# A 31-tap depthwise convolution on one engine in place of two

## The reference, cut to what matters

```python
def conformer_conv_mixer(h_conv, dw_w, dw_b, ln_g, ln_b):
    a, g = jnp.split(h_conv, 2, axis=-1)          # 256 channels each
    u = a * jax.nn.sigmoid(g)
    u = depthwise_conv(u, dw_w, dw_b)             # 31 taps per channel
    return jax.nn.silu(layernorm(u, ln_g, ln_b))
```

## Time and profile before

| | |
|---|---|
| median of 3 runs | 3576.89 us (3570.51 to 3579.43) |
| profiled execution | 3579.76 us, span of its trace 3577.9 us |
| TensorE matmul busy | 3313.3 us, 93% |
| VectorE busy | 1830.2 us, 51% |
| GpSimd busy | 1969.5 us, 55% |
| ScalarE busy | 758.2 us, 21% |
| mean granted TensorE clock | 0.965 of full |

### The profile page before, as it was taken

One profiled execution on the slowest core, in us unless ns is written; L12 is line 12 of the kernel. 1 busy time (PEld: TensorE's weight loads), 2 busy tenths in 40 slices (PEclk: granted clock), 3 DMA queues, 4 the chain that ended last, 5 costly groups with the idle time before them and its releaser, 6 DMA issues.

```text
span 3577.9 us, 44532 instructions
## 1 busy us (share of the span) xinstructions
PE 3313.3 (93%) x14288; PEld 2588.7 (72%) x14288; DVE 1830.2 (51%) x2038; ACT 758.2 (21%) x1269; POOL 1969.5 (55%) x1148
## 2 busy tenths in 40 slices
PE   7999997799999999996889999888898899999997
PEld 5888773378887788874457888667776777778886
DVE  6641367653313743157654331765668766853313
ACT  2110124422201111013432210211123222222201
POOL 4556654356666546665426666533344445666664
PEclk9999998899999999998899999989999999999998
DMA  4223320023333223330013332312122122233332
GB/s 138 77 83 94 112 71 12 7 72 98 96 98 112 89 71 95 94 106 30 12 36 94 94 99 94 103 53 64 59 68 65 59 71 71 86 92 100 94 95 76
DMA packets 77136, 280.89 MB, mean 79 GB/s; under 512 B 9350, under 2 KB 9734, under 8 KB 76360
## 3 DMA queue, kind: packets, MB, share of 16 engines
q1 hardware_dynamic: 74016, 268.84, 24.6%
q10 hardware_dynamic: 2984, 10.27, 0.9%
HBM read 276.97 MB, written 2.10 MB: 78 GB/s over the span
## 4 chain that ended last, share of the span: by engine, by line
PE 78%; DVE 15%; issue 4%; ACT 2%; DVEq 0%; ACTq 0%; POOL 0%; DMA 0%; SPq 0%; POOLq 0%
PE bank L547 23%; PE bank L552 23%; PE bank L551 23%; DVE y L1872 1%; DVE xbc L2164 1%; PE bank L811 1%; PE bank L672 1%; DVE x_lo L1630 1%; PE bank L829 1%; PE bank L754 1%; DVE ssm_lo L1784 1%; DVE square_sum L1640 1%; DVE scaled L1994 1%; PE bank L742 1%; PE bank L1027 1%
## 5 line engine op out<-in xcount | busy, mean ns | idle before, releaser
L447 POOL TENSOR_SCALAR w_hi<-raw 128x1024 fp32r<-128x1024 f32 x504 | 554.6, 1100 | 1523.2 <-PE bank L547 1514.4
L450 POOL TENSOR_TENSOR w_lo<-raw,w_hi 128x1024 fp32r<-128x1024 f32 x504 | 1266.1, 2512 | 42.0
L547 PE MATMUL bank<-x_hi,w_hi 128*128 128x512 f32 x2896 | 1159.7, 400 | 86.7 <-DVE x_lo L1630 30.0
L551 PE MATMUL bank<-x_lo,w_hi 128*128 128x512 f32 x2896 | 1141.8, 394 | 0.0
L552 PE MATMUL bank<-x_hi,w_lo 128*128 128x512 f32 x2896 | 1141.5, 394 | 0.0
L547 PEld LDWEIGHTS bank<-x_hi,w_hi 128*128 128x128 f32 x2896 | 553.0, 191 | 228.7 <-issue 99.9
L551 PEld LDWEIGHTS bank<-x_lo,w_hi 128*128 128x128 f32 x2896 | 553.5, 191 | 119.3 <-issue 5.1
L552 PEld LDWEIGHTS bank<-x_hi,w_lo 128*128 128x128 f32 x2896 | 552.2, 191 | 118.1
L552 PE MATMUL bank<-hidden_hi,w_lo 128*128 (+1 forms) x880 | 347.6, 395 | 0.0
L547 PE MATMUL bank<-hidden_hi,w_hi 128*128 (+1 forms) x880 | 347.6, 395 | 0.0
L551 PE MATMUL bank<-hidden_lo,w_hi 128*128 (+1 forms) x880 | 347.6, 395 | 0.0
(11 more groups left out here) (373 smaller groups left out, 3407.0 us busy)
## 6 DMA issues: line engine op xcount, KB each, us to landing
raw<-in_w SPq DMA_DIRECT2D x504, 512.0 KB, 3.6
dft<-in_dft ACTq DMA_DIRECT2D x2, 1536.0 KB, 6.9
x<-in_x SPq DMA_DIRECT2D x2, 1024.0 KB, 6.6
out<-x SPq DMA_DIRECT2D x4, 512.0 KB, 2.6
mask<-in_mask ACTq DMA_DIRECT2D x1, 1536.0 KB, 8.2
filt_cos<-in_dft_filter ACTq DMA_DIRECT2D x2, 512.0 KB, 6.1
filt_sin<-in_dft_filter ACTq DMA_DIRECT2D x2, 512.0 KB, 7.2
sel<-in_sel ACTq DMA_DIRECT2D x1, 768.0 KB, 4.4
```

Source lines behind the costliest of these rows:

```text
L447: nc.gpsimd.tensor_scalar(w_hi[:, s % 2, :], raw[:, s, :], 1.0, 0.0, ALU.mult, ALU.add).then_inc(w_rounded, 1)
L450: nc.gpsimd.tensor_tensor(w_lo[:, s % 2, :], raw[:, s, :], w_hi[:, s % 2, :].bitcast(F32), ALU.subtract).then_inc(w_split, 1)
L547: first = nc.tensor.matmul(out, hi_w, hi, start=start, stop=False)
L551: nc.tensor.matmul(out, hi_w, lo, start=False, stop=False)
```

## The change

GpSimd no longer computes any tap: `long_conv`, its two semaphores and the scratch tiles go, and GpSimd's list for the whole program up to the second block is weight splits alone. VectorE computes all 62 taps of a layer, alternating between the two tiles: tap number n belongs to tile n % 2, and waits for the previous tap of its own tile, for which `tap_at` now has two entries. `maximum` issues two taps behind each row maximum while there are any, and its scaling waits for the maximum alone and no longer for a tap. `fold` and `spectrum_sums` still issue one. `branches_done` no longer waits for GpSimd. The loop over the layers counts 180 steps of `dve_step` in place of 149.

```diff
-    "dve": {"pair_free": 44, "tile_free": 14, "dve_step": 149, "x_rounded": 24, "x_split": 24, "x_squared":
+    "dve": {"pair_free": 44, "tile_free": 14, "dve_step": 180, "x_rounded": 24, "x_split": 24, "x_squared":
...
-        tap_products = (rstd[:], latent[:, 2, :])
...
-            def long_conv(l, first, end):
...
-                def tap(j):
-                    return issue(nc.gpsimd.tensor_scalar(tap_products[j % 2], long_pad[:, 0, j:j + T],
-                                                         layer_cols[:, CONV_W + j:CONV_W + j + 1], 0.0,
-                                                         ALU.mult, ALU.add))
...
-                for j in range(first, end):
-
-                    pool.wait_ge(long_tap, added)
-                    this = product
-                    if j + 1 < end:
-                        product = tap(j + 1)
-                    pool.wait_ge(long_tap, max(this, added))
-                    added = issue(nc.gpsimd.tensor_tensor(acc, acc, tap_products[j % 2], ALU.add))
...
-            for l in range(LAYERS):
-
-                end = l * LAYER_BLOCKS + FFN_BLOCKS + IN_BLOCKS + 2
-                split_blocks(at, end)
-                long_conv(l, 0, TAPS // 2)
-                split_blocks(end, end + 2)
-                long_conv(l, TAPS // 2, TAPS)
-                at = end + 2
-
...
-                taken, tap_at = [0], [None]
+                taken, tap_at = [0], [None, None]

                 def long_tap():

-                    j = taken[0]
+                    i, j = taken[0] % 2, taken[0] // 2
                     taken[0] += 1
                     if j:
-                        dve.wait_ge(dve_step, tap_at[0])
-                    acc, w, src = conv_acc[:, 1, :], col(CONV_W + TAPS + j), long_pad[:, 1, j:j + T]
+                        dve.wait_ge(dve_step, tap_at[i])
+                    acc, w, src = conv_acc[:, i, :], col(CONV_W + i * TAPS + j), long_pad[:, i, j:j + T]
                     if j == 0:
-                        ins = nc.vector.tensor_scalar(acc, src, w, col(CONV_B + 1), ALU.mult, ALU.add)
+                        ins = nc.vector.tensor_scalar(acc, src, w, col(CONV_B + i), ALU.mult, ALU.add)
                     else:
                         ins = nc.vector.scalar_tensor_tensor(acc, src, w, acc, ALU.mult, ALU.add)
                     ins.then_inc(dve_step, c.add(dve_step))
-                    tap_at[0] = c.at(dve_step)
+                    tap_at[i] = c.at(dve_step)

                 def tap():
-                    if taken[0] < TAPS:
+                    if taken[0] < 2 * TAPS:
                         long_tap()
...
-                def maximum(h, t, tap=True):
+                def maximum(h, t):
                     dve.wait_ge(scores_ready, c.next(scores_ready))
                     nc.vector.reduce_max(row_shift[:, t:t + 1], bank[SCORE_BANKS[(4 * h + t) % 3]][:], AX_X
                                          ).then_inc(dve_step, c.add(dve_step))
-                    if tap and taken[0] < TAPS:
-                        long_tap()
-                    dve.wait_ge(dve_step, c.at(dve_step))
+                    reduced = c.at(dve_step)
+                    tap()
+                    tap()
+                    dve.wait_ge(dve_step, reduced)
                     nc.vector.tensor_scalar(row_shift[:, t:t + 1], row_shift[:, t:t + 1],
                                             -QK ** -0.5, None, ALU.mult).then_inc(row_ready, c.add(row_ready))
...
-                while taken[0] < TAPS:
+                while taken[0] < 2 * TAPS:
                     long_tap()
-                dve.wait_ge(dve_step, tap_at[0])
+                dve.wait_ge(dve_step, tap_at[1])

                 def branches_done():
                     y_update(1, 0)
-                    dve.wait_ge(long_done, c.next(long_done))
                     dve.sem_inc(ln_in, 1)
```

More of the change, by code:

```diff
@@ L110 @@
            "q_ready": 8, "q_roped": 8, "scores_ready": 32, "row_ready": 40, "probs_ready": 32,
-           "mixed_ready": 8, "mixed_copied": 8, "long_done": 1, "spec_free": 4, "filt_loaded": 48,
-           "odd_copied": 8, "spec_taken": 4, "k_copied": 4},
+           "mixed_ready": 8, "mixed_copied": 8, "spec_free": 4, "filt_loaded": 48, "odd_copied": 8,
+           "spec_taken": 4, "k_copied": 4},
 }
@@ L389, in build @@
         gate_in, gate_out = sem("gate_in"), sem("gate_out")
-        long_tap, long_done = sem("long_tap"), sem("long_done")
         norm_in, norm_squared, norm_summed, norm_sum, norm_rms, norm_scaled, norm_rounded, norm_split = (
@@ L461, in split_blocks @@
                     split_block(n, n // RAW, n % RAW, True)
-            def long_conv(l, first, end):
[L465 to L472, removed]
-                def tap(j):
-                    return issue(nc.gpsimd.tensor_scalar(tap_products[j % 2], long_pad[:, 0, j:j + T],
-                                                         layer_cols[:, CONV_W + j:CONV_W + j + 1], 0.0,
-                                                         ALU.mult, ALU.add))
[L479 to L487, removed]
-                for j in range(first, end):
-                    pool.wait_ge(long_tap, added)
-                    this = product
-                    if j + 1 < end:
-                        product = tap(j + 1)
-                    pool.wait_ge(long_tap, max(this, added))
-                    added = issue(nc.gpsimd.tensor_tensor(acc, acc, tap_products[j % 2], ALU.add))
-                pool.wait_ge(long_tap, added)
-                if end == TAPS:
-                    pool.sem_inc(long_done, 1)
             for n in range(RAW):
```

## The result

| | before | after |
|---|---|---|
| median | 3578.16 us (3570.51 to 3582.34, 4 runs) | 3557.06 us (3553.68 to 3561.33, 4 runs) |
| profiled execution | 3579.76 us, span 3577.9 | 3557.09 us, span 3555.3 |
| ratio, 95% interval | | 0.9948 (0.9934 to 0.9962) |

By the medians that is 21.1 us or 0.6% less, by the ratio 18.6 us or 0.5%. Two repetitions beside the experiments gave 14.4 us less (ratio 0.9957, 0.9941 to 0.9973) and 17.2 us less (0.9953, 0.9941 to 0.9966). One of the six executions of the second repetition took 11595 us; the ratio leaves it out, and without it that median is 3559.20 and not 3559.34. The forecast was 14.2 us less, 3563 us, in a range of 3554 to 3571.

The account below looks back on a forecast made before the run. TensorE was busy 93% of the span, but GpSimd's work stretched VectorE's instructions in the attention heads; steps sum to -8.8 us per layer, +1.7 for a slow clock spell, -14.2 for both layers: 3563 us, range 3554 to 3571.

Parts of the forecast that it names:

- rival D: Stretched VectorE instructions are not GpSimd's doing: 12.3 us lost per layer, 3601.5 us; chance 0.05.
- Step (1): Query rotations, two rounds: eight sums fall from 0.93 to 0.69 us each, 1.9 us saved per layer.
- Step (2): Maxima of score head 0: 9.50 us becomes 8.34, 1.2 us saved per layer.
- Steps (3) and (7): head(0) and head(4): first reduce to last scaling falls from 18.76 and 20.66 to 14.07 us, saving 4.7 and 6.6.
- Step (4): head(1): three second taps ahead of the spectrum TensorE waits for, 1.3 us lost per layer.
- Step (5): head(2): four second taps, each ahead of a `y_update` or the exponentials, 1.7 us lost per layer.
- Step (6): head(3): TensorE's transform and ScalarE's copy set its end and the maxima have slack; no change beyond the rotations.
- Step (8): head(5), which had no taps: slower first pitch and later scalings of the second and third maxima, 2.6 us lost.
- C: Each second tap costs the full 0.90 us, as if waited for: +3.5 us per layer, 3584 us; chance 0.06.
- E: VectorE isn't the whole path in head(0) and head(4), half their saving goes: 3574 us; chance 0.07.
- A: TensorE's clock holds in head(5), or slow spells elsewhere vanish: 3559 us, or 3556 with one fewer per layer; chance 0.17.
- B: More slow TensorE clock spells, as waits in head(2) grow: one more per layer 3566 us, two 3569.5; chance 0.17.

Follow-up runs that it names:

- without taps on GpSimd: Kernel before with one of GpSimd's 31 tile-0 taps kept and 30 left out of the computation, VectorE's taps and waits as before: 3539.96 us, ratio 0.9901.
- the busy GpSimd beside the changed kernel: Changed kernel with GpSimd's 61 instructions per layer put back on scratch tiles, result unused: 3609.13 us, ratio to before 1.0098.
- the kernel with 62 taps in waits: Changed kernel with its 62 taps laid elsewhere, many where VectorE waits, up to six together, some ahead of query rotations: 3531.87 us, ratio to before 0.9885.

## Why the prediction was right

The sum was right within the scatter (-14.2 against -14.4, -17.2 and -21.1 us) and so was the mechanism: silence on GpSimd shortens VectorE's instructions, the second taps give part of it back. That the sum came so close is partly luck, because both of these terms were too large. Below, the sizes of the steps, for one layer. Lengths of heads are from first maximum to first maximum in the first layer, of before, then of the three profiles of the changed kernel.

- **The silence.** Forecast by rival D's arithmetic: 19.4 us, of them 0.95 in the first round of rotations, which lies ahead of the stretch. Measured without taps on GpSimd: 16.8 by half the whole time, and 14.6 and 14.0 in the two stretches, for 18.4. The parts at head(0) and head(4) were right in the first layer (6.4 and 8.3 forecast, 6.4 and 8.1 measured); score head 0 gave 1.9 and not 2.8, because its fourth maximum then waits 1.08 us for TensorE, and head(3) and head(5) lost 2.6 together. In the second layer head(4) gave only 6.2, head(1) lost 1.2, and head(3) and head(5) lost nothing: before the change, head(3) and head(4) share their 41 us differently in the two layers (14.59 + 26.44 and 16.15 + 24.67).
- **Step (1)**, the rotation sums: 0.68 us each after, as against the 0.93 of the earlier trace rows, 2.0 us for 1.9 forecast.
- **Step (2)**: 8.51 us (538.72 to 547.23) for 8.34. The shorter pitch was eaten by the 0.55 us for which the fourth reduce waits for TensorE's scores. 1.0 us saved for 1.2.
- **Steps (3) and (7)**: 13.77 us each for 14.07. The heads fell from 24.54 to 19.3 or 19.5 us and from 26.44 to 19.5: 5.0 to 5.3 saved for 4.7, 6.9 for 6.6.
- **Step (4)**, head(1): from 19.57 to 20.4 to 21.0, 0.9 to 1.5 lost for 1.3. **Step (5)**, head(2) with the rotations behind it: from 29.78 to 30.7 or 30.8, 0.9 to 1.1 lost for 1.7 - 0.95 = 0.75, though with a spell at the lower clock level that wasn't in the sum. **Step (6)**, head(3): unchanged, 14.5, except for the 17.55 us of the second layer in one of the three profiles.
- **Step (8)** and the clock, head(5): from 16.12 to 20.1, 4.0 lost for 2.6 + 1.7 = 4.3. The wait was to be 3.4 us and is 3.82, and the transform takes 5.38.
- **The price of a second tap** is the term of the sum that was mis-sized. I had it at 0.42 us; it is 1.98 - 1.72 = 0.26, since only the 0.24 ahead of the scaling was credited to the dropped wait, and the 0.22 behind it was taken for a fixed cost though it holds 0.16 of the wait too. Against the kernel without taps on GpSimd (first layer of the first repetition), the five parts with 19 second taps, score head 0 and heads 0, 1, 2 and 4, grew by 6.2 us together; 8.0 were forecast, and 19 x 0.26 is 4.9. Head(5), where maxima without a tap got two each, grew by 2.9 (4.0 in the second layer) for 4.3 forecast with the clock. Head(3) got shorter by 1.6, where nothing was forecast; why is not shown. Together 134.89 - 127.36 = 7.5 us for 12.3. (27 x 0.26 is 7.0 too, but that is chance: the heads don't grow by it.)
- **How the two errors met.** In the stretch, silence was over by 18.4 - 14.6 = 3.8 us and the second taps by 4.8. What is left is 6.1 forecast (7.1 less the 0.95 ahead of the stretch) and 7.1 measured. In the three profiles' six stretches the saving was 6.5 to 7.2 us in five and 3.3 in the one with a second slow spell in head(3).
- **The rivals.** C is excluded for this code by the pitch of 1.98 us, D by the busy GpSimd beside the changed kernel, E by 13.77 us in head(0) and head(4), with their chain whole on VectorE. A fell with the 5.38 us in head(5). B is seen in part: one spell more per layer, at the start of head(3) (604.80), in all six stretches of the three profiles and in neither of before.
- **The rule of the Trainium skill** on waits between Vector instructions (VectorE: DVE Perf Modes, The DRAIN you can't avoid) doesn't hold for this kernel's semaphore waits: with nothing else changed, waiting for the taps costs 0.40 us per maximum and 24.4 us in all. The same section does say that a next instruction that isn't held back starts earlier, which fits the 0.66. The page's advice to issue fewer instructions (Rules for kernel authors) holds behind the maxima, where 30 taps cost 35.0 us, and not for taps laid in waits, where 62 took as long as 32. The rule on the shared port (SBUF — State Buffer, Who interferes with whom) agrees with the runs here as to which instructions stretch each other, and that it can be either engine's. It says that the pair is held for the whole instruction; here GpSimd's split lasted from 593.20 to 597.03 and the run of taps until 596.12, so it was held through the rest of the run and not for one tap.
- **The covered steps.** The moved splits cost nothing that shows in the changed kernel: in its profile, no matmul of the two stretches waited for a split. They are not harmless as such: in the kernel with 62 taps in waits the four taps at 521.28 met the first of them, too, and took 7.78 us for 2.7.
- **What isn't the change's.** The 21.1 us of the first comparison lie 4 to 7 above the two repetitions. The profiled pair differs by 22.7 us, but its stretches only by 6.9 + 3.3, and the first rounds of rotations, ahead of them, by 1.2 and 1.3. The other 10 lie in stages with the same code, 6 of them in the second block, where two executions of the changed kernel also came out 6 us apart. What an edit's size is must be read from its own stretch and from several runs.

## What to carry to other kernels

Before work moves from GpSimd to VectorE, look for VectorE instructions with two SBUF inputs that have two lengths in the trace: the longer ones are the price of having both engines at work, here 14 to 17 us a layer. Then ask of each added instruction where it waits and what waits for it: behind a row maximum it cost its 0.66 us in most heads (and the pair 0.40 more if the scaling waited for it), but nothing in the head whose end TensorE and ScalarE set. With most taps where VectorE waits for TensorE or ScalarE, 30 more of them cost 0.5 and 0.1 us in the two stretches. Beside weight splits four taps took nearly three times their length (7.78 us for 2.7), or the split nearly four times its own (3.83 for 1.04). The kernel with the same 62 taps on VectorE took from 3583.67 down to 3522.34 us, by their places and one wait.

## What the runs showed of the hardware that was not expected

- The gap behind a scaling isn't fixed. VectorE's timeline of the kernel with 62 taps in waits, head(0), where no tap stands behind these maxima and every scaling had to wait for its reduce:

```profile
548.11 0.69 DVE L1918 TENSOR_REDUCE row_shift<-bank 128x1 f32<-128x512 f32 x1
548.95 0.15 DVE L1923 TENSOR_SCALAR row_shift<-row_shift 128x1 f32<-128x1 f32 x1
549.17 0.69 DVE L1918 TENSOR_REDUCE row_shift<-bank 128x1 f32<-128x512 f32 x1
550.01 0.15 DVE L1923 TENSOR_SCALAR row_shift<-row_shift 128x1 f32<-128x1 f32 x1
550.08 0.41 DVE L1858 TENSOR_TENSOR square<-folded,spectrum 128x256 f32<-128x256 f32 x1
```

  From a scaling that had waited it is 0.22 us to a reduce, which has a wait of its own, and 0.07 to a product, which by the code has none. In the changed kernel, where the scaling didn't have to wait any more, it is 0.06 to a reduce too. That fits a queue which gets past the next wait while VectorE is still busy with taps, and can't while it stands in a wait itself; that this is the cause wasn't tested by itself.
- The engine that comes second pays, and for a whole run of instructions. A tap sequence already running held GpSimd's rounding split, so that it took 3.83 us in place of 1.04, while the taps themselves kept 0.66 us each; four other taps, that met two splits, took 7.78 us.
- Executions of one kernel differ in stages that no edit touched. The profiles of the two repetitions, taken on different chips, are 10.1 us apart in span (3547.6 and 3557.7), with the attention stretches alike within 0.3 us; the six executions of the first repetition, on one chip, ran from 3549.41 to 3562.02 us.
